# Block 2's mixer: a pair's weights normalised ahead of the next scores, projections in another order around the attention

## The reference, cut to what matters

```
zx = modulate(rms_norm(x, norm_g[l, 1]), mx[3], mx[4]) @ w_in[l]
qa, ka, va, qb, kb, vb, ux, gx = split_combined(zx)
qb, kb = rope(qb), rope(kb)
ya = neighborhood_attention(qa, ka, va, ka_c, va_c, na_rpb[l], rows)   # branch a, 6 heads of 64
yb = window_attention(qb, kb, vb, kb_c, vb_c, sw_sink[l])             # branch b, 6 heads of 64
yc = conformer_conv(ux, ...)       # a * sigmoid(gate), 31-tap convolution, layer norm, silu
ga, gb, gc = split(sigmoid(gx + b_gate[l]), 3)
x = x + mx[5] * ((ga * (ya @ w_oa) + gb * (yb @ w_ob) + gc * (yc @ w_oc)) @ w_o)
```

## Time and profile before

| | us |
|---|---|
| median of 3 runs | 2594.11 |
| the profiled execution, and its span | 2609.25, 2607.5 |
| TensorE busy | 2384.9 (91% of the span) |
| VectorE busy | 1576.0 (60%) |
| ScalarE busy | 875.2 (34%) |
| GpSimd busy | 236.8 (9%) |
| HBM | 329.78 MB read, 127 GB/s over the span |

### The profile page before, as it was taken

How to read it: one execution, slowest core, us unless ns; L and a number is a source line. 1 busy time by engine, 2 the same in 40 slices (tenths; PEclk the granted TensorE clock), 3 DMA queues, 4 the chain that set the end, 5 groups by cost and what they waited for, 6 DMA issues and landing times.

```text
span 2607.5 us, 32546 instructions
## 1 busy us (share of the span) xinstructions
PE 2384.9 (91%) x12934; PEld 2004.2 (77%) x12934; DVE 1576.0 (60%) x2902; ACT 875.2 (34%) x1494; POOL 236.8 (9%) x321
## 2 busy tenths in 40 slices
PE   5998897899999986889999999999999997789998
PEld 4788776788888754568888888888888885578998
DVE  4886886577766336554469976654333355666665
ACT  3344343322223333333332222232222233335443
POOL 1000001100001200002211111100000120012001
PEclk9898998899999997889999999999999998899999
DMA  6543542355443310112336665523222241134553
GB/s 231 173 145 115 170 146 81 105 186 169 162 164 111 105 52 17 45 51 84 109 104 220 217 210 205 190 69 101 89 97 92 86 126 57 59 113 156 186 184 124
DMA packets 95351, 332.96 MB, mean 128 GB/s; under 512 B 11040, under 2 KB 13216, under 8 KB 94816
## 3 DMA queue, kind: packets, MB, share of 16 engines
q1 hardware_dynamic: 70496, 244.41, 27.8%
q0 software_dynamic: 23376, 84.80, 10.0%
q10 hardware_dynamic: 1328, 1.66, 0.2%
HBM read 329.78 MB, written 2.48 MB: 127 GB/s over the span
## 4 chain that ended last, share of the span: by engine, by line
PE 81%; DVE 12%; issue 3%; ACT 3%; POOL 1%; DMA 1%; ACTq 0%; POOLq 0%; DVEq 0%
PE PS L460 79%; DVE WL L1128 2%; PE PS L767 2%; DVE ST L1141 2%; ACT WH L834 1%; DVE NT L1137 1%; DVE HL L1137 1%; DVE CV L1137 1%; DVE JK L1138 1%; DVE AR L1138 1%; DVE P L1132 1%; DVE PJ L1137 0%; DVE PS L1128 0%; DMA CST<-in_cst 0%; POOL SS L1717 0%
## 5 line engine op out<-in xcount | busy, mean ns | idle before, releaser
L834 ACT ACTIVATE WH<-RAW 128x1024 fp32r<-128x1024 f32 (+2 forms) x482 | 494.5, 1027 | 1095.8 <-PE PS L460 1095.6
L460 PE MATMUL PS<-HH,WH 128*128 128x512 f32 (+1 forms) x2136 | 769.6, 360 | 14.0 <-DVE HL L1137 6.9
L460 PE MATMUL PS<-HH,WL 128*128 128x512 f32 (+1 forms) x2136 | 758.5, 355 | 0.0
L460 PE MATMUL PS<-HL,WH 128*128 128x512 f32 (+1 forms) x2136 | 758.5, 355 | 0.0
L1128 DVE TENSOR_TENSOR WL<-RAW,WH 128x1024 fp32r<-128x1024 f32 (+2 forms) x482 | 572.3, 1188 | 187.6 <-ACT WH L834 186.6
L460 PEld LDWEIGHTS PS<-HH,WH 128*128 128x128 f32 x2136 | 413.9, 194 | 88.2 <-issue 12.8
L460 PEld LDWEIGHTS PS<-HH,WL 128*128 128x128 f32 x2136 | 413.5, 194 | 58.2
L460 PEld LDWEIGHTS PS<-HL,WH 128*128 128x128 f32 x2136 | 414.4, 194 | 57.0
L460 PE MATMUL PS<-GH,WH 128*128 128x512 f32 (+1 forms) x776 | 271.1, 349 | 0.0
L460 PE MATMUL PS<-GL,WH 128*128 128x512 f32 (+1 forms) x776 | 270.1, 348 | 0.0
L460 PE MATMUL PS<-GH,WL 128*128 128x512 f32 (+1 forms) x776 | 270.1, 348 | 0.0
(11 more groups left out here) (218 smaller groups left out, 2945.7 us busy)
## 6 DMA issues: line engine op xcount, KB each, us to landing
RAW<-in_wst SPq DMA_DIRECT2D x420, 512.0 KB, 3.4
AR<-in_w_adaT POOLq DMA_DIRECT2D x144, 512.0 KB, 3.7
RAW<-in_wst SPq DMA_DIRECT2D x48, 384.0 KB, 3.0
BM<-rpb_rows POOLq DMA_DIRECT2D x48, 64.0 KB, 2.9
CB<-in_cc POOLq DMA_DIRECT2D x2, 1024.0 KB, 8.8
RAW<-in_wst SPq DMA_DIRECT2D x8, 256.0 KB, 2.8
RAW<-in_wst SPq DMA_DIRECT2D x4, 396.0 KB, 5.4
rpb_rows<-in_rpb POOLq DMA_DIRECT2D x2, 697.5 KB, 10.1
```

The lines of the kernel that those rows point to most:

```text
L460: return e.matmul(o, l, r, start=start, stop=stop)
L834: return e.activation(o, i, f, bias=bias, scale=scale)
```

## The change: what it does, and the diff

In the `B` step of VectorE reciprocal and scaling of job i - 1 stand ahead of the additions and maxima of job i; on ScalarE the copy of the transposed weights of job i - 1 stands ahead of the exponential of job i. TensorE's `B` step is as before. `mixer` starts the attention after fewer dense steps, and lays one rope step and at most one `B` step between whole dense steps; the stretch without dense steps is gone. The first four gates are computed before the first product, and a product stands two gates ahead of the place it had. Gates have four places in the new `MG`; `UT`, `RT2` and `LT` take over what `TM2` held. No arithmetic is added or taken away. `nb` is 14 in layer 0 and 8 in layer 1.

```diff
@@ mixer
-        if last:
-            feat(w, l, 384, 3, "qa", "H", norm, 512, 3, halves=BOTH)
-            feat(w, l, 0, 3, "qa", "H", norm, nq, 0)
-        else:
-            feat(w, l, 0, 3, "qa", "H", norm, nq, 0, halves=BOTH)
-            feat(w, l, 384, 3, "qa", "H", norm, 512, 3)
+        qa((3, 4, 5) if last else (3, 0, 4), BOTH)
+        if last:
+            qa((0,), ((0, nq),))
         tokm(w, l, ((768, 1152), (1664, 1792)), (2, 2, 2, 2), "v2", "H", norm, 4, (0, 1, 2, 3))
-        out += mix(D=7) + ["K"]
-        feat(w, l, 1792, 2, "ua", "H", norm, nq)
-        feat(w, l, 2048, 2, "ub", "H", norm, nq)
+        out += mix(D=5 if last else 4) + ["K"]
+        for i in (1, 2) if last else (1, 5, 2):
+            qa((i,), ((0, 512 if i > 2 else nq),))
...
         for i in range(4):
+            feat(w, l, 1792 + 128 * i, 1, "ua" if i < 2 else "ub", "H", norm, nq, i % 2)
             ropes[l, i] = T[tile("rope", l, i, 256)]
+        gates(0, 0, 1, 2, 3)
         nb = 3 * nq // 128 + 2
-        b0 = nb // 2
-        out += mix(D=4, B=b0 // 2)
-        out += mix(D=4, B=b0 - b0 // 2, C=4)
-        out += ["F"] + mix(B=nb - b0, P=4, C=9)
...
-        out += mix(D=12, B=nb, C=18)
-        out += mix(D=12, L=3 * nq // 128)
-        out += mix(D=12)
+        nu = 6 if last else 7
+        b0 = round(nb * nu / (nu + 8))
+        b1 = round(nb * 4 / (nu + 8))
+        out += mix(D=nu, B=b0)
+        for i in range(4):
+            out += ["D", "D", "P"] + ["B"] * ((b1 * (i + 1)) // 4 - b1 * i // 4)
+        out += mix(D=4, B=nb - b0 - b1, C=6)
+        for b in range(3):
+            product(b, 0)
+            gates(b, 4, 5)
+            product(b, 2)
+            gates(b, 6, 7)
+            product(b, 4)
+            if b < 2:
+                gates(b + 1, 0, 1)
+            product(b, 6)
+            if b < 2:
+                gates(b + 1, 2, 3)
+        out += ["F"] + mix(D=12, B=nb, C=17) + ["F"]
+        out += mix(D=5, C=8)
+        out += mix(D=7, L=3 * nq // 128)
+        out += mix(D=8)
@@ temporaries
-    TM2 = at("TM2", 130.5, [128, 3, 512])
+    UT = at("UT", 98, [128, 3, 512])
+    RT2 = at("RT2", 96, [128, 256])
-    MT = at("MT", 48, [128, 4, 512])
+    LT = at("LT", 48, [128, 2, 512])
+    MT = at("MT", 52, [128, 2, 512])
+    MG = at("MG", 128.5, [128, 4, 512])
@@ vector_program, attention2 (scalar_program moves the copy to PT2 in the same way)
                     for i in range(n + 2):
+                        j = i - 1
+                        if 0 <= j < n:
...
+                            e.reciprocal(Y, Z).then_inc(*vb.inc("r", l, br, j))
...
+                                ts(P, P, Y[:, a:a + 1], None, ALU.mult, None).then_inc(*vb.inc("n", l, br, j, a))
                         if i < n:
                             p, x = jobs[i]
```

More of the change, by code:

```diff
@@ L165, in mixer, with qa, gates, product @@
         w = "w_in_2"
-        if last:
-            feat(w, l, 384, 3, "qa", "H", norm, 512, 3, halves=BOTH)
-            feat(w, l, 0, 3, "qa", "H", norm, nq, 0)
-        else:
-            feat(w, l, 0, 3, "qa", "H", norm, nq, 0, halves=BOTH)
-            feat(w, l, 384, 3, "qa", "H", norm, 512, 3)
+        def qa(tiles, halves):
+            passes([(unit((w, l, 0, 8, ((128 * i, 128 * i + 128),)), "f", "H", norm), "qa", l, i) for i in tiles], halves)
+        def gates(b, *tiles):
+            for i in tiles:
+                c = 2304 + 1024 * b + 128 * i
+                passes([(unit((w, l, 0, 8, ((c, c + 128),)), "f", "H", norm), f"gt{b}", l, i)], ((0, nq),))
+        def product(b, i):
+            name, kn = (("w_out_a_2", 3), ("w_out_b_2", 3), ("w_out_c_2", 2))[b]
+            S.append(Step(unit((name, l, 0, kn, ((128 * i, 128 * i + 256),)), "f", "Y2", l, 3 * b), 0, nq,
+                          [tile(f"ob{b}", l, i, nq), tile(f"ob{b}", l, i + 1, nq)]))
+        qa((3, 4, 5) if last else (3, 0, 4), BOTH)
+        if last:
+            qa((0,), ((0, nq),))
         tokm(w, l, ((768, 1152), (1664, 1792)), (2, 2, 2, 2), "v2", "H", norm, 4, (0, 1, 2, 3))
-        out += mix(D=7) + ["K"]
-        feat(w, l, 1792, 2, "ua", "H", norm, nq)
-        feat(w, l, 2048, 2, "ub", "H", norm, nq)
+        out += mix(D=5 if last else 4) + ["K"]
+        for i in (1, 2) if last else (1, 5, 2):
+            qa((i,), ((0, 512 if i > 2 else nq),))
         for j in range(3):
@@ L1064, in attention2 @@
                     for i in range(n + 2):
+                        j = i - 1
+                        if 0 <= j < n:
+                            x = jobs[j][1]
+                            kt = keys2(x)[1]
+                            c = slice(128 * (x % 2), 128 * (x % 2) + 128)
+                            for a in range(2):
+                                q.wait_ge(*pb.at("t", l, br, j, a))
+                                if x % 2 == 0 and (j or br):
+                                    q.wait_ge(*pb.at("v", l, *((br, j - 1) if j else (0, n - 1))))
+                                af(PT2[:, a, 0:kt, c], heads(PS[6 + a][:, 0:128 * kt], 128), ACT.Copy).then_inc(
+                                    *ab.inc("pt", l, br, j, a))
                         if i < n:
@@ L1078, in attention2 @@
                                         *ab.inc("sink", l, i, a))
[L1079 to L1089, removed]
                         j = i - 2
@@ L1221, in evictions @@
                     elif x.kind == "ub":
-                        V = TM2[:, 2, 0:n]
+                        V = UT[:, 2, 0:n]
                         q.wait_ge(*ad.at("ub", l, i))
@@ L1232, in evictions @@
                         q.wait_ge(*ad.at("gt", l, 0, i))
-                        stt(ACC[:, i, 0:n], MT[:, i % 2, 0:n], 1.0, P[:, 0:n], ALU.add, ALU.mult).then_inc(*vd.inc("ev", d))
+                        stt(ACC[:, i, 0:n], MG[:, i % 4, 0:n], 1.0, P[:, 0:n], ALU.add, ALU.mult).then_inc(*vd.inc("ev", d))
                         vd.same("ob", l, 0, i)
@@ L1532, in attention2 @@
                     for i in range(n + 2):
+                        j = i - 1
+                        if 0 <= j < n:
+                            g = 2 * (n * br + j)
+                            Z, Y = ST2[:, 64 + g:66 + g], ST2[:, 128 + g:130 + g]
+                            if br:
+                                q.wait_ge(*ab.at("sink", l, j, 1))
+                                tt(Z, Z, ST2[:, 192 + 2 * j:194 + 2 * j], ALU.add).then_inc(*vb.inc("z", l, j))
+                                q.wait_ge(*vb.at("z", l, j))
+                            else:
+                                q.wait_ge(*ab.at("exp", l, br, j, 1))
+                            e.reciprocal(Y, Z).then_inc(*vb.inc("r", l, br, j))
+                            q.wait_ge(*vb.at("r", l, br, j))
+                            nk = 128 * keys2(jobs[j][1])[1]
+                            for a in range(2):
+                                P = P2[:, 2 * (j % 2) + a, 0:nk]
+                                ts(P, P, Y[:, a:a + 1], None, ALU.mult, None).then_inc(*vb.inc("n", l, br, j, a))
                         if i < n:
@@ L1555, in attention2 @@
                                 ts(M, M, SM[:, 56 + h:57 + h], None, ALU.min, None).then_inc(*vb.inc("m", l, br, i, a))
[L1556 to L1571, removed]
                         j = i - 2
@@ L1740, in evictions @@
                             q.wait_ge(*gd.at("acc", l, 1, i))
-                        tt(ACC[:, i, 0:n], ACC[:, i, 0:n], MT[:, 2 + i % 2, 0:n], ALU.add).then_inc(*gd.inc("acc", l, br, i))
+                        tt(ACC[:, i, 0:n], ACC[:, i, 0:n], MT[:, i % 2, 0:n], ALU.add).then_inc(*gd.inc("acc", l, br, i))
                     elif x.kind == "o0":
```

38 lines of the change are left out of this document (15 added, 23 removed).

## The result

The changed kernel takes 2511.32 us (median of 4 runs, 2509.53 to 2515.68) against 2593.65 for the kernel before in the same series: a ratio of 0.9685, 95% interval 0.9665 to 0.9706, 82 us faster. The forecast was 2501 us, its range 2465 to 2550. The profiled execution took 2515.68 us (span 2513.9) against 2609.25: 93.6 us less, where the sum had said 93. The medians differ by less; the part on the prediction comes back to this.

A forecast was written before the change was run, and what follows sets the result against it. TensorE in the attention stretches was taken as held by transposes waiting for VectorE's scaling and by a lowered clock. 72 + 31 - 5 - 5 = 93 us gave 2516 profiled, 2501 at the median; range 2465 to 2550.

The forecast's parts named there:

- VectorE late by its order, not its load; scaling ahead hides the wait: Both attention stretches: transposes wait 2.6 us each for `P`; scaling before the next scores lets TensorE's own work cover it.
- The plan without a stretch lacking dense work: Layer 0, 980 to 1024 us, TensorE busy 26.71 of 44 us at 0.70 clock; part of the waits, not counted again.
- Waits 93.5 to 21 us: Transposes waiting for `P`: 5 us left in layer 0, 11 in layer 1, 5 at rope steps; gain 72 us.
- ScalarE's copy ahead costs nothing: The copy moved before the exponential in a `B` step is over about when the maxima are: no cost.
- The clock: 50 us of loss fall to 19: TensorE's granted clock in both attention stretches recovers as gaps shrink to less than a quarter; gain 31 us, bounds 0 and 50.
- Rival 1: The clock does not come back because microsecond gaps remain at half of the jobs: 62 us gain, 2532 us; chance 15%.
- Layer norm 5 us: Layer norm in 7 dense steps instead of 12: its 3.1 us chain nearly covered; 3 us lost in layer 0, 2 in layer 1.
- Last products back to back 5 us: TensorE waits for the last merged tiles before w_o: new waits of 2.7 and 2.6 us, bounds 0 and 8.
- The sum: Gains 72 and 31 less costs 5 and 5: 93 us, from 2609.25 to 2516 profiled, 2501 at the median.
- Rival 2: VectorE's order keeps half of the waits, scaling standing behind splits, taps and `YL`: 59 us gain, 2535 us; chance 14%.
- Rival 3: Scaling stands behind a weight split waiting for `WH`, 3.6 us at each of 36 places: 65 us slower, 2660; chance 4%.

The follow-up runs named there:

- YL late: Changed kernel with VectorE's `YL` of job i - 2 put one `B` step later, the last of a branch excepted: 2497.46 us, ratio 0.9617.
- rope and tail mended: Changed kernel with `YL` one step later, rope step behind its `B` step, branch c's last gate between the last two products: 2484.64 and 2479.72 us in two groups.
- the plan alone: Changed kernel with the old order inside a `B` step on VectorE and ScalarE; new plan, gate places and temporaries kept: 2576.89 us, ratio 0.9931.
- the order alone: Kernel before, with its old plan and buffers, given the new `attention2` order on VectorE and ScalarE: 2526.39 us, ratio 0.973.

## Why the prediction was right, and where its sizes were off

*VectorE late by its order, not its load; scaling ahead hides the wait.* Right. Undoing this order alone brings back 84.5 of the 93.5 us of waits and 65 of the 82 us.

*The plan without a stretch lacking dense work.* Its waits had been counted in the same sum. Shown apart: 18 us alone, 12 to 17 on top of the order.

*Waits 93.5 to 21 us.* Measured 35.5; this is the term that was mis-sized. Its parts: rope 5 forecast, 6.0 measured; layer 0 elsewhere 5 forecast, 12.8 measured; layer 1 elsewhere 11 forecast, 16.7 measured. The prediction set the time from an exponential to its scaling (4 us) against TensorE's cover, and named the stop at `YL` only in passing. What counts is the list: VectorE stands at `YL`, 4.00 and 4.12 us at the two longest waits of layer 1, and then owes everything that stands between. Moving it made 10.5 us of waits and some 14 us of time.

*ScalarE's copy ahead costs nothing.* Nearly so: 2.7 us of waits, no time that could be told.

*The clock: 50 us of loss fall to 19.* In the profiled executions it fell further. By the prediction's own terms, layer 0: 223.2 us less 206 of work and 17.1 of waits leaves nothing, though the clock was 0.98; layer 1: 137.6 less 113, 18.4 and 1.6 of other waits leaves 5. The work terms were some 4 and 1 us too large (a dense matmul was taken at 0.24 us, and they start 0.23 apart): with YL late, at a granted 1.00, TensorE was busy for 201.84 us with the same 994 matmuls, and with rope and tail mended for 111.9 us in layer 1 at 0.99. By these the loss was 54 us and fell to 10. The gain is much the same either way, 44 or 45 instead of 31. Rival 1, the clock that stays low, fell. The share of the stretch that TensorE sat idle, and the clock it was granted, over the kernels of this case in layer 0: 22% and 0.85, 18% and 0.92 (the plan alone), 13% and 0.94 (the order alone), 8% and 0.98 (changed), 6% and 1.00 (YL late). In layer 1 it was 25% and 0.81, 22% and 0.91, 19% and 0.91, 15% and 0.94, 11% and 0.97. The Trainium skill, "TensorE: Matmul & The Clock Gate", section "A second HAM failure mode: psum-queue depth-cycling", tells of one kernel in which short idle times between groups of matmuls were frequent enough to make the clock swing; it does not say that any gap does, as the prediction read it. The kernels with most idle time agree with the page, and gaps of up to 2.3 us at ten jobs (YL late, layer 0) came with a granted 1.00.

*Layer norm 5 us.* Measured 0.3 + 0.8 us of waits for `LT` where there were 1.6: no cost. The chain of 3.1 us was covered.

*Last products back to back 5 us.* Measured 2.2 and 2.5 us, 4.1 more than the 0.6 before; the forecast places were 2.7 and 2.6. Right.

*Not foreseen:* in layer 1 a wait of 0.9 us for `YL` at the first product behind branch b, 0.4 for `CV`, 1.0 for `UT` at a rope step, 0.6 of scores for the exponential.

*The sum.* 100.5 us in the attention stretches, less 4.1 (`ML`), plus 0.5 at the layer norm, less 1.3 (`YL` and `CV`), is 95.6; the profiled executions differ by 93.6. That the forecast of 93 fits this pair is luck: the waits gave 14 us less than forecast (58 instead of 72), the clock 13 to 14 more.

*The median.* From 2593.65 the forecast 93 would have given 2501; the medians differ by 82. The prediction took the profiled execution's distance to the median, 15.1 us, as lasting; behind the change it is 4.4. The runs suggest where it comes from. Of 27 executions of the kernel before in the three groups of experiments the 13 fastest took 2590 to 2598 us at a mean granted clock of 0.954 to 0.959, the other 14 took 2601 to 2606 us at 0.950 to 0.954; the profiled one took 2609.25 us at 0.951. So its trace seems to hold more loss by the clock than the median execution, and the 11 us between 93.6 and 82 would be part of the gain of 44. Without them the clock gives an estimated 33 us, close to the forecast 31, and the 10 us by which the median missed the forecast are in the main the waits, the term that was mis-sized. This is argued, since the kernel before has one trace only.

*Rival 2*, half of the waits stay, had its mechanism right and its size wrong: 38% stayed, with the lower clock gone all the same. *Rival 3*, slower by a scaling behind the weight split: the first job shows the split at 894.92 without a wait and the scaling right behind it; no stretch got slower.

## What to carry to other kernels

When the engine that others wait for is itself half idle, look at what stands behind what on its list, not at its load: an instruction whose inputs are long there belongs ahead of one that waits for the other engine. After such a move look for the next instruction at which that engine stands still (here `YL` and the rope): everything behind it is late by as much, and moving it one step was worth another 14 us. And when short waits on TensorE are removed, count the granted clock too; here it gave back nearly as much as the waits did (44 us beside 58 in the profiled pair, an estimated 33 by the medians). Look also at where the profiled execution lies among the others: what it has above the median is in every loss read from its trace.

## What the runs showed of the hardware that was not expected

The sum of the gaps does not fix the granted clock. The plan alone had 49.7 us of waits in layer 0 where the kernel before had 54.8, in a stretch of 270 instead of 250 us, and was granted 0.92 instead of 0.85. At the same idle share, 22%, layer 0 of the kernel before was granted 0.85 and layer 1 of the plan alone 0.91. Why, no run here tells: the places of the gaps differ, 165 matmuls more lie between them in layer 0, and executions of one kernel differ in the clock too (0.950 to 0.959 over the whole span for the kernel before). Nor does the mean over the span fix the time: one of the four executions of the plan alone was granted 0.914 and took 2583.98 us, 7 to 8 us more than the others at 0.963 and 0.964.
